# First two up-projection pairs of the feed-forward run on un-normed rows, with root and shift applied after the matmul

## The chip, the cores and the metric

The kernel runs on one core of one Trainium2 chip. The metric is the device time of one execution in microseconds (us), lower is better. Engines are named as in the profile: PE (TensorE; PEld its weight loads), DVE (VectorE), ACT (ScalarE), POOL (GpSimd), SP (SyncE, which issues the weight DMAs here).

## The reference, cut to what matters

The reference computes two transformer layers on 256 tokens of width 1024 in float32. Only the end of the second layer is touched:

```
x = x + gate_a * ((g_a * o_a + g_b * o_b) @ w_o)
h = rms_norm(x, ffn_norm) * (1.0 + scale_f) + shift_f
u = conv_width_3(h @ w_up) + b_conv          # causal, per channel, 2 * 2816 channels
val, gt = split(u, 2)
x = x + gate_f * ((silu(gt) * val) @ w_down)
```

`rms_norm` multiplies every token's row by one root, 1 / sqrt(mean of squares + eps), and every channel by a gain. The root is one number for each token, the gain times (1 + scale) and the shift one number for each channel. So `h @ w_up` equals root * ((x * gain) @ w_up) + shift @ w_up.

## The kernel before, in words

Activations lie transposed: `hT` is the residual stream as 8 tiles (KT = 8) of 128 channels x 256 tokens. Weights come as 512 KB tiles (128 x 1024) through a ring of 6 slots, `wring`, which SP fills in order; a slot is refilled once the tile six places before is done. Every float32 product is made of three faster ones. ACT rounds a weight tile into `whi` (`act_hi`, line 478, ring of 3), DVE subtracts to get the rest `wlo` (`tile_lo`, line 483, ring of 6), and PE runs upper x upper, upper x rest, rest x upper (`three`, lines 489 to 491): 24 matmuls of 256 columns for a tile. The normed activations are split likewise into `xhi`, `xlo` (both in `xboth`). POOL can run `tile_lo` too, and does so in two earlier stages.

The stage before the change is the output projection `w_o`, 8 tiles. PE makes tile t in one of 3 banks (`pe_w_o`); for each tile m DVE adds the result to `hT` (`dve_residual`, line 1662) and releases the bank (`ring_free`), ACT then rounds the weight tile three places ahead and squares `hT[m]` (`act_w_o`, lines 478 and 532), DVE makes that tile's rest (`low_ahead`), and PE sums squares over channels with a matmul against ones (`norm_sum`, line 543).

Then the norm: the last three sums; 22 matmuls on constants to keep PE busy (`pe_warm`, line 539; 44 records); ACT takes the root of the mean (`norm_act`, line 559), DVE the reciprocal (`norm_root`, 563), DVE scales 8 tiles of `hT` by it (`norm_scale`, 567), ACT applies gain and shift (571) and rounds (577), DVE makes the rests two tiles at a time (`x_rest_pair`, 597). PE starts the first up pair when the first two tiles are split (`split_pair`, called in `up_first`).

The feed-forward has FT = 22 turns. Tiles in order (F0 is the first): up pair of turn 0 (F0, F0+1), up pair of turn 1 (F0+2, F0+3), down tile of turn 0 (F0+4), up pair of turn 2 (F0+5, F0+6), down of turn 1 (F0+7), and so on. In a turn ACT copies both up results out of PSUM (`z`, 2684), DVE applies the convolution (`one`: two at 2740, four at 2748), ACT takes silu (2690), DVE multiplies value and gate into upper and rest (2758, 2759, 2761), which releases the turn's down tile on PE by the semaphore `f_w`. The engines' queues are in order, and every wait is on a semaphore written out by hand; nothing reorders work.

## Time and profile before

| | us |
|---|---|
| median of 3 runs | 1693.74 |
| range of the runs | 1693.2 to 1695.26 |
| span of the profiled execution | 1692.3 |
| median less span (what lies around it) | 1.4 |
| PE busy in the span | 1638.4 (97%) |
| DVE busy | 1244.8 (74%) |
| ACT busy | 825.3 (49%) |
| POOL busy | 157.1 (9%) |

The profile is of one execution. Times in rows count from the start of its span. In a timeline a row is: start, duration, engine, line and operation, output and inputs, shapes, count (xN: N records merged), and in brackets the idle time of that engine just before with what released it. A merged row's duration runs from the first start to the last end. Successive instructions on DVE and ACT overlap at their ends, so the step from start to start is shorter than a duration.

### The profile page before, as it was taken

To read this page: it belongs to the slowest core of one execution; us is meant where nothing else is said; L and a number is where in the kernel's file an instruction comes from. 1 tells how busy PE (TensorE), PEld (TensorE's weight loads), DVE (VectorE), ACT (ScalarE), POOL (GpSimd) and SP (SyncE) were. 2 spreads that over 40 slices of the span, in tenths; PEclk is the share of its full clock that TensorE was granted. 3 is DMA by queue.
4 is the path that set the end of the run, shared out by engine and by line. 5 is a ranking of instruction groups with operands and counts; after the bars stand their busy time and mean duration, and the time that the engine had idled before them with its cause. 6 is when DMAs were issued, how large, how long until landed. Compare 5 with 4: busy or idle time off the path is not lost.

```text
span 1692.3 us, 32795 instructions
## 1 busy us (share of the span) xinstructions
PE 1638.4 (97%) x11656; PEld 1442.0 (85%) x11656; DVE 1244.8 (74%) x2601; ACT 825.3 (49%) x1495; POOL 157.1 (9%) x131
## 2 busy tenths in 40 slices
PE   6999999999999999999999999999999988999998
PEld 4887977899988887888888888887999766899998
DVE  6885538639989888788888887887345665678887
ACT  3544011344469844555555555555444246454443
POOL 0020000007700000000000000000007203200000
PEclk9999999999999999999999999999999999999999
DMA  8742136665741388677777777776554560145553
GB/s 346 283 144 88 40 127 232 258 199 177 221 141 60 111 265 263 228 232 235 237 236 237 236 236 232 240 233 207 160 184 146 182 205 2 63 135 179 183 185 125
DMA packets 102621, 316.93 MB, mean 187 GB/s; under 512 B 11392, under 2 KB 21376, under 8 KB 102144
## 3 DMA queue, kind: packets, MB, share of 16 engines
q1 hardware_dynamic: 101664, 311.27, 56.5%
q10 hardware_dynamic: 864, 4.39, 0.7%
q8 instruction: 62, 1.02, 0.2%
q14 instruction: 31, 0.25, 0.1%
HBM read 309.71 MB, written 5.90 MB: 186 GB/s over the span
## 4 chain that ended last, share of the span: by engine, by line
PE 67%; DVE 11%; ACT 9%; issue 8%; DMA 3%; POOL 2%; DVEq 0%; SPq 0%; ACTq 0%; POOLq 0%
PE bank L489 9%; PE bank L491 9%; PE bank L490 9%; PE bank L1943 4%; PE bank L504 4%; PE bank L1945 4%; PE bank L1947 4%; PE bank L1206 3%; ACT whi L478 3%; PE bank L505 2%; ACT arena L1906 2%; PE bank L464 2%; PE bank L1492 2%; ACT arena L1897 2%; DVE xn L2065 2%
## 5 line engine op out<-in xcount | busy, mean ns | idle before, releaser
L483 DVE TENSOR_TENSOR wlo<-wring,whi 128x1024 fp32r<-128x1024 f32 x350 | 426.4, 1223 | 104.2 <-ACT whi L478 95.3
L478 ACT CAST whi<-wring 128x1024 fp32r<-128x1024 f32 x392 | 409.9, 1046 | 116.4 <-PE bank L1947 49.5
L489 PE MATMUL bank<-xboth,whi 128*128 128x256 f32 x1232 | 353.9, 287 | 7.9 <-DVE wlo L483 2.7
L490 PE MATMUL bank<-xboth,whi 128*128 128x256 f32 x1232 | 348.5, 283 | 0.0
L491 PE MATMUL bank<-xboth,wlo 128*128 128x256 f32 x1232 | 348.5, 283 | 0.0
L489 PEld LDWEIGHTS bank<-xboth,whi 128*128 128x128 f32 x1232 | 236.2, 192 | 13.1 <-issue 5.6
L490 PEld LDWEIGHTS bank<-xboth,whi 128*128 128x128 f32 x1232 | 236.3, 192 | 0.7 <-issue 0.5
L491 PEld LDWEIGHTS bank<-xboth,wlo 128*128 128x128 f32 x1232 | 236.2, 192 | 0.0
L504 PE MATMUL bank<-xboth,whi 128*128 128x512 f32 x616 | 220.8, 397 | 0.0
L483 POOL TENSOR_TENSOR wlo<-wring,whi 128x1024 fp32r<-128x1024 f32 x42 | 109.1, 2601 | 884.1 <-ACT whi L478 884.1
L505 PE MATMUL bank<-xboth,wlo 128*128 128x256 f32 x616 | 172.7, 280 | 0.0
L1943 PE MATMUL bank<-whi,Whi 128*128 128x512 f32 x512 | 159.4, 392 | 3.0 <-DVE Wlo L2048 3.0
L1945 PE MATMUL bank<-wlo,Whi 128*128 128x512 f32 x512 | 158.6, 391 | 0.0
L1947 PE MATMUL bank<-whi,Wlo 128*128 128x512 f32 x512 | 157.7, 389 | 0.0
L504 PEld LDWEIGHTS bank<-xboth,whi 128*128 128x128 f32 x616 | 115.7, 188 | 27.5
L505 PEld LDWEIGHTS bank<-xboth,wlo 128*128 128x128 f32 x616 | 116.3, 189 | 3.4
L1943 PEld LDWEIGHTS bank<-whi,Whi 128*128 128x128 f32 x512 | 95.5, 188 | 21.9 <-issue 3.9
L1945 PEld LDWEIGHTS bank<-wlo,Whi 128*128 128x128 f32 x512 | 96.1, 188 | 21.1
L1947 PEld LDWEIGHTS bank<-whi,Wlo 128*128 128x128 f32 x512 | 96.1, 188 | 21.1
L2007 ACT COPY arena<-bank 128x256 f32<-128x256 f32 x88 | 32.9, 373 | 133.6 <-PE bank L508 133.6
L2057 DVE TENSOR_TENSOR arena<-arena 128x256 f32<-128x256 f32 x88 | 56.0, 637 | 52.4 <-ACT arena L2009 52.4
L2009 ACT ACTIVATE arena<-arena 128x256 f32<-128x256 f32 x88 | 36.8, 418 | 81.7 <-DVE arena L2054 81.7
(378 smaller groups left out, 2709.0 us busy)
## 6 DMA issues: line engine op xcount, KB each, us to landing
wring<-in_w SPq DMA_DIRECT2D x463, 512.0 KB, 3.9
arena<-in_ada SPq DMA_DIRECT2D x48, 512.0 KB, 6.8
xn<-in_ada SPq DMA_DIRECT2D x96, 256.0 KB, 3.1
h_spill<-arena SPq DMA_DIRECT2D x37, 128.0 KB, 1.9
arena<-h_spill SPq DMA_DIRECT2D x37, 128.0 KB, 4.0
wring<-in_w SPq DMA_DIRECT2D x6, 384.0 KB, 4.0
wring<-in_w SPq DMA_DIRECT2D x8, 256.0 KB, 3.3
arena<-in_const ACTq DMA_DIRECT2D x1, 1215.0 KB, 5.5
```

Source lines behind the costliest of these rows:

```text
L478: act.copy(whi[:, n % HSLOTS, :], wring[:, n % SLOTS, :]).then_inc(hi_ready, 1)
L483: eng.tensor_tensor(wlo[:, n % SLOTS, :], wring[:, n % SLOTS, :], whi[:, n % HSLOTS, :].bitcast(F32), ALU.subtract).then_inc(lo_ready, 1)
L489: pe.matmul(out, h, xh, start=start, stop=False, **kw)
L490: pe.matmul(out, h, xl, start=False, stop=False, **kw)
L491: return pe.matmul(out, l, xh, start=False, stop=stop, **kw)
L504: pe.matmul(out, h, xboth[:, k, :, :], start=(k == 0), stop=False)
L505: pe.matmul(out[:, 0:S], l, xhi[:, k, :], start=False, stop=False)
L1206: mm = pe.matmul(bank[r % BANKS][:, 0:S], blocks(tile % SLOTS, k), xn[:, k, :], start=(k == 0), stop=(k == KT - 1))
L1943: pe.matmul(tok_accs[b][f][:, :], Wh, h[:, f * 512:(f + 1) * 512], start=first, stop=False)
L1945: pe.matmul(tok_accs[b][f][:, :], Wh, l[:, f * 512:(f + 1) * 512], start=False, stop=False)
L1947: mm = pe.matmul(tok_accs[b][f][:, :], Wl, h[:, f * 512:(f + 1) * 512], start=False, stop=last)
L2057: dve.tensor_tensor(ge[:, b, :], ge[:, b, :], g, ALU.mult).then_inc(w_gated, 1)
```

## The change

For turns 0 and 1 the up projection no longer waits for the norm. In the `w_o` stage ACT makes `hT[m] * gain` rounded (`raw_upper`) and DVE its rest (`raw_rest`) for each tile m, into a new buffer `raw3` with 258 columns a tile; the last two columns hold the shift, so that the matmul also gives shift @ w_up. PE runs the pairs of turn 0 (`up_first`, banks 1 and 3) and turn 1 (`up_second`, banks 0 and 2) on `raw3`; the two last `norm_sum` stand in the middle of `up_first`, and the 22 constant matmuls are gone. DVE multiplies the results by the root on the way out of PSUM (`z_scale`) and ACT adds the shift (`z_shift`). The normed rows are made after that, by one DVE instruction a tile (`norm_gain`), one on ACT (`norm_upper`) and one on DVE (`norm_rest`), between the pieces of turn 0; they are first used by turn 2. The rests of the weight tiles F0+4 and F0+5 move from DVE to POOL, and the silu table is loaded right after the root. Banks of the later turns are swapped.

```diff
@@ pe_w_o, act_w_o
-            for m in (KT - 2, KT - 1):
-                norm_sum(pe, 3, m, nsq[3])
-            pe_warm(pe, 7, 22)
         def act_w_o(act):
             for m in range(KT):
                 act.wait_ge(ring_free, RING0["w_o"] + m + 1)
+                if m == 0:
+                    raw_shift_upper(act, raw3, 9)
+                raw_upper(act, raw3, 3, m, 3 * KT)
...
+        def raw_shift_upper(act, raw, shift):
+            act.copy(raw[:, :, 0, S:RAW], wide(modc(shift, 0, KT), 2))
+        def raw_upper(act, raw, n, m, at):
+            act.activation(raw[:, m, 0, 0:S], hT[:, m, :], ACT.Identity, scale=gsc[:, n, m:m + 1]).then_inc(x_hi, 1)
+        def raw_rest(dve, raw, n, m, at):
+            dve.wait_ge(x_hi, at + m + 1)
+            dve.scalar_tensor_tensor(raw[:, m, 1, 0:S], hT[:, m, :], gsc[:, n, m:m + 1], raw[:, m, 0, 0:S].bitcast(F32),
+                                     ALU.mult, ALU.subtract).then_inc(x_lo, 1)
+        def norm_gain(dve, n, k, rt):
+            dve.scalar_tensor_tensor(xn[:, k, :], hT[:, k, :], gsc[:, n, k:k + 1], rt, ALU.mult,
+                                     ALU.mult).then_inc(x_scaled, 1)
+        def norm_upper(act, n, k, shift):
+            act.wait_ge(x_scaled, KT * n + k + 1)
+            act.activation(xhi[:, k, :], xn[:, k, :], ACT.Identity, bias=modc(shift, k)).then_inc(x_hi, 1)
+        def norm_rest(dve, k, shift, at):
+            dve.wait_ge(x_hi, at + k + 1)
+            dve.scalar_tensor_tensor(xlo[:, k, :], xn[:, k, :], modc(shift, k), xhi[:, k, :].bitcast(F32), ALU.add,
+                                     ALU.subtract).then_inc(x_lo, 1)
@@ pe_ffn
             def up_first():
                 pe.wait_ge(lo_ready, nth_split[F0 + 1])
-                split_pair(pe, (bank[0][:, 0:S], bank[0][:, S:2 * S], False), F0, 3)
+                pe.wait_ge(ring_free, RING0["w_o"] + KT - 2)
+                for k in range(KT):
+                    if k == 4:
+                        for m in (KT - 2, KT - 1):
+                            norm_sum(pe, 3, m, nsq[3])
+                    pe.wait_ge(x_lo, 12 + k + 1)
+                    for i in range(2):
+                        mm = three(pe, bank[1 + 2 * i][:, 0:RAW], F0 + i, k, raw3[:, k, 0, :], raw3[:, k, 1, :], k == 0, k == KT - 1)
...
+            def up_second():
+                pe.wait_ge(ring_free, RING0["w_o"] + KT)
+                for i in range(2):
+                    n = up_tile(1) + i
+                    pe.wait_ge(lo_ready, nth_split[n])
...
             up_first()
-            up(1, 0)
+            up_second()
             down(0, 0, first=True)
+            pe.wait_ge(x_lo, 12 + 2 * KT)
@@ act_ffn
+            def z_shift(f):
+                act.wait_ge(z_scaled, f + 2)
+                for k in range(2):
+                    ins = act.activation(zf[:, f, k, 2:258], zf[:, f, k, 2:258], ACT.Identity,
+                                         bias=z_add[:, 2 * f + k:2 * f + k + 1])
+                ins.then_inc(f_z, 1)
...
+            for k in range(4):
+                norm_upper(act, 3, k, 9)
             hi(F0 + 3, 0)
-            act.wait_ge(pad_ready, 1)
-            turn(0)
-            turn(1)
+            z_shift(0)
+            hi(F0 + 4, 0)
+            for k in range(4, KT):
+                norm_upper(act, 3, k, 9)
+            silu(0, 0)
+            hi(F0 + 5, 0)
+            z_shift(1)
+            hi(F0 + 6, 0)
+            silu(1, 0)
@@ dve_ffn
+            def z_scale(f):
+                dve.wait_ge(tile_done, up_tile(f) + 2)
+                for k in range(2):
+                    dve.tensor_tensor(zf[:, f, k, 2:258], bank[1 - f + 2 * k][:, 0:S], rtn[3], ALU.mult)
+                    ins = dve.tensor_copy(z_add[:, 2 * f + k:2 * f + k + 1], bank[1 - f + 2 * k][:, S:S + 1])
+                ins.then_inc(z_scaled, 1)
...
+                if between:
+                    between()
+                if f == 1:
+                    dve.wait_ge(lo_ready, nth_split[F0 + 5])
...
+            for k in range(4):
+                norm_gain(dve, 3, k, rtn[3])
             lo(F0 + 3, 0)
-            one(0, 0)
+            z_scale(0)
+            for k in range(4, KT):
+                norm_gain(dve, 3, k, rtn[3])
+            for k in range(4):
+                norm_rest(dve, k, 9, 4 * KT)
...
+            one(0, 0, rest)
+            z_scale(1)
             one(1, 0)
@@ scalar, vector, gpsimd programs
             act_w_o(act)
+            act_hi(act, F0 + 2, count_at(F0 + 2), None)
             norm_act(act, 3, rtn[3])
-            act_hi(act, F0 + 2, count_at(F0 + 2), None)
-            norm_shift_split(act, 3, 9)
+            act_table(act, ACT.Silu)
...
             def low_ahead(m):
                 n = FIRST["w_o"] + HSLOTS + m
...
-                if n < F0 + 1:
+                if n < F0 + 2:
                     tile_lo(dve, n, nth_split[n])
+                if m == 0:
+                    dve.wait_ge(x_hi, 3 * KT + 1)
+                    raw_shift_rest(dve, raw3, 9)
+                raw_rest(dve, raw3, 3, m, 3 * KT)
             dve_residual(dve, "w_o", 8, beside=low_ahead)
-            tile_lo(dve, F0 + 1, nth_split[F0 + 1])
+            tile_lo(dve, F0 + 2, nth_split[F0 + 2])
             norm_root(dve, v, 3, rtn[3])
-            norm_scale(dve, rtn[3])
-            for k in range(0, KT, 2):
-                x_rest_pair(dve, 3, k)
-                if k == 2:
-                    tile_lo(dve, F0 + 2, nth_split[F0 + 2])
...
+            pool.wait_ge(lo_ready, nth_split[F0 + 3])
+            for n in (F0 + 4, F0 + 5):
+                tile_lo(pool, n, nth_split[n])
```

The function called `rest` in `one(0, 0, rest)` makes `norm_rest` for the tiles 4 to 7; `one` calls it after its convolution and before the product with silu.

## Rows read from the trace of the kernel before

**Rows 1.** Windows: stretch, length, busy time of each engine (count), PEclk granted clock, DMA.

```profile
core 0: us, PE busy (x) PEld busy (x) DVE busy (x) ACT busy (x) POOL busy (x), PEclk, DMA share, GB/s
1487.30:1494.90 7.60, 6.58 (x51) 5.89 (x50) 6.83 (x12) 4.80 (x11) 0.00 (x0) 1.00 0.25 72
1526.00:1680.00 154.00, 154.00 (x1286) 154.00 (x1285) 125.42 (x216) 71.56 (x91) 0.00 (x0) 1.00 0.56 175
```

**Rows 2.** Timeline of PE from the last sums to the down tile of turn 1.

```profile
1487.25 1.03 PE L543 MATMUL bank<-arena,keep 128*128 128x256 f32 x4
...
1488.97 5.07 PE L539 MATMUL bank<-keep 128*128 128x128 f32 x44
1494.99 0.36 PE L489 MATMUL bank<-xboth,whi 128*128 128x256 f32 x1 [0.94 <-DVE xboth L597]
...
1508.77 0.39 PE L489 MATMUL bank<-Whi,whi 128*128 128x256 f32 x1 [1.66 <-DVE wlo L483]
...
1511.75 0.28 PE L489 MATMUL bank<-xboth,whi 128*128 128x256 f32 x1
...
1517.51 0.28 PE L489 MATMUL bank<-Whi,whi 128*128 128x256 f32 x1
```

**Rows 3.** Timelines of DVE and ACT, first tile of the output projection.

```profile
1465.19 0.48 DVE L1662 SCALAR_TENSOR_TENSOR hT<-bank,mod,hT 128x256 f32<-128x256 f32 x1 [0.76 <-PE bank L491]
1466.79 1.23 DVE L483 TENSOR_TENSOR wlo<-wring,whi 128x1024 fp32r<-128x1024 f32 x1 [1.11 <-ACT whi L478]
...
1465.71 1.05 ACT L478 CAST whi<-wring 128x1024 fp32r<-128x1024 f32 x1 [1.85 <-DVE hT L1662]
```

**Rows 4.** Timelines of DVE and ACT, last residual tile and norm.

```profile
1487.45 0.48 DVE L1662 SCALAR_TENSOR_TENSOR hT<-bank,mod,hT 128x256 f32<-128x256 f32 x1 [2.82 <-PE bank L491]
...
1489.68 1.75 DVE L563 RECIPROCAL arena<-arena 128x256 f32<-128x256 f32 x1 [0.48 <-ACT arena L559]
1491.47 2.77 DVE L567 TENSOR_TENSOR xn<-hT,arena 128x256 f32<-128x256 f32 x8
...
1489.17 0.47 ACT L559 ACTIVATE arena<-bank,cols 128x256 f32<-128x256 f32 x1 [0.79 <-PE bank L543]
1489.55 1.03 ACT L478 CAST whi<-wring 128x1024 fp32r<-128x1024 f32 x1
```

**Rows 5.** Timeline of DVE, turn 0 of the feed-forward.

```profile
1502.17 1.22 DVE L483 TENSOR_TENSOR wlo<-wring,whi 128x1024 fp32r<-128x1024 f32 x1 [3.02 <-ACT whi L478]
1503.31 0.73 DVE L2740 TENSOR_SCALAR arena<-arena,cols 128x256 f32<-128x256 f32 x2
1504.08 1.80 DVE L2748 SCALAR_TENSOR_TENSOR arena<-arena,cols 128x256 f32<-128x256 f32 x4
1506.36 0.43 DVE L2758 TENSOR_TENSOR Whi<-arena 128x256 fp32r<-128x256 f32 x1 [0.48 <-ACT arena L2690]
...
1507.16 0.43 DVE L2761 TENSOR_TENSOR Wlo<-arena,Whi 128x256 fp32r<-128x256 f32 x1
```

**Rows 6.** One line's instructions: durations ns min/median/max, first and last start.

```profile
L2068 DVE COPY mod<-part x96: 153/154/157, 596.1 to 1171.7; 128x1 f32 x87, 128x1 f32<-128x1 f32 x9
```

**Rows 7.** DVE line 2195, then POOL's timeline in the same stretch (1303 to 1311).

```profile
L2195 DVE SCALAR_TENSOR_TENSOR arena<-arena,cols x5: 474/1643/2628, 1303.3 to 1308.3; 128x256 f32<-128x256 f32 x5
...
1302.31 2.40 POOL L483 TENSOR_TENSOR wlo<-wring,whi 128x1024 fp32r<-128x1024 f32 x1 [3.71 <-ACT whi L478]
1305.18 2.47 POOL L483 TENSOR_TENSOR wlo<-wring,whi 128x1024 fp32r<-128x1024 f32 x1 [0.48 <-ACT whi L478]
1308.07 2.53 POOL L483 TENSOR_TENSOR wlo<-wring,whi 128x1024 fp32r<-128x1024 f32 x1 [0.42 <-ACT whi L478]
```

**Rows 8.** PE's timeline and windows (columns as in rows 1) around gaps elsewhere.

```profile
1390.83 0.90 PE L670 MATMUL bank<-keep,arena 128*128 128x128 f32 x3 [2.31 <-POOL arena L783]
1419.94 0.90 PE L670 MATMUL bank<-keep,arena 128*128 128x128 f32 x3 [1.25 <-POOL arena L783]
...
1388.00:1390.00 2.00, 0.51 (x3) 0.11 (x1) 1.89 (x12) 0.95 (x6) 0.05 (x1) 0.80 0.00 0
1394.00:1396.00 2.00, 2.00 (x11) 1.85 (x10) 0.49 (x6) 2.00 (x6) 0.57 (x2) 0.50 0.00 0
1396.00:1398.00 2.00, 2.00 (x13) 1.42 (x12) 0.91 (x7) 2.00 (x9) 0.83 (x2) 0.99 0.02 4
1422.00:1424.00 2.00, 2.00 (x13) 1.86 (x13) 0.68 (x7) 0.99 (x6) 0.33 (x1) 0.67 0.00 0
```

More of the change, by code:

```diff
@@ L166 @@
 ARENA = 41920
+RAW = S + 2
+RAW3_AT = 18736
 AFTER_WHI = S * NK + 2 * KT * S + HSLOTS * D
@@ L2634, in act_w_o, with raw_shift_rest @@
                 act_square(act, 3, m, nsq[3])
+        z_add = arena[:, RAW3_AT + 2 * KT * RAW + S:RAW3_AT + 2 * KT * RAW + S + 4]
+        def raw_shift_upper(act, raw, shift):
+            act.copy(raw[:, :, 0, S:RAW], wide(modc(shift, 0, KT), 2))
+        def raw_upper(act, raw, n, m, at):
+            act.activation(raw[:, m, 0, 0:S], hT[:, m, :], ACT.Identity, scale=gsc[:, n, m:m + 1]).then_inc(x_hi, 1)
+        def raw_shift_rest(dve, raw, shift):
+            dve.tensor_tensor(raw[:, :, 1, S:RAW], wide(modc(shift, 0, KT), 2), raw[:, :, 0, S:RAW].bitcast(F32), ALU.subtract)
+        def raw_rest(dve, raw, n, m, at):
[12 more added lines that the diff above has]
+                                     ALU.subtract).then_inc(x_lo, 1)
         f_z, f_u, f_g, f_whi, f_w = sem("f_z"), sem("f_u"), sem("f_g"), sem("f_whi"), sem("f_w")
@@ L2647, in up_first @@
                 pe.wait_ge(lo_ready, nth_split[F0 + 1])
-                split_pair(pe, (bank[0][:, 0:S], bank[0][:, S:2 * S], False), F0, 3)
+                pe.wait_ge(ring_free, RING0["w_o"] + KT - 2)
[6 more added lines that the diff above has]
+                        mm = three(pe, bank[1 + 2 * i][:, 0:RAW], F0 + i, k, raw3[:, k, 0, :], raw3[:, k, 1, :], k == 0, k == KT - 1)
+                        if k == KT - 1:
+                            mm.then_inc(tile_done, 1)
+            def up_second():
[3 more added lines that the diff above has]
+                    pe.wait_ge(lo_ready, nth_split[n])
+                    for k in range(KT):
+                        mm = three(pe, bank[2 * i][:, 0:RAW], n, k, raw3[:, k, 0, :], raw3[:, k, 1, :], k == 0, k == KT - 1)
+                    mm.then_inc(tile_done, 1)
             def up(f, i):
@@ L2724, in lo, with one @@
                     tile_lo(dve, n, 6 * i + nth_split[n])
-            def one(f, i):
+            def z_scale(f):
[4 more added lines that the diff above has]
+                ins.then_inc(z_scaled, 1)
+            def one(f, i, between=None):
                 n = turn_tile(f)
-                if f > 0:
+                if f > 1:
                     lo(n + 2, i)
@@ L2761, in one, with rest @@
                 dve.tensor_tensor(Wlo[:, b, :], Wf[:, b, :], Whi[:, b, :].bitcast(F32), ALU.subtract).then_inc(f_w, 1)
+            for k in range(4):
+                norm_gain(dve, 3, k, rtn[3])
             lo(F0 + 3, 0)
-            one(0, 0)
+            z_scale(0)
[3 more added lines that the diff above has]
+                norm_rest(dve, k, 9, 4 * KT)
+            def rest():
+                for k in range(4, KT):
+                    norm_rest(dve, k, 9, 4 * KT)
+            one(0, 0, rest)
+            z_scale(1)
             one(1, 0)
```

16 lines of the change are left out of this document (10 added, 6 removed).

## Prediction

> **What bounds the kernel now.** I read the page first: PE is busy for 97% of the span and no other engine is near that. Then the windows by stage [rows 1]. In the loop of the feed-forward PE is busy 154.0 of 154.0 us while DVE has 125.4, so a shift of PE's schedule at the entry of the loop reaches the end one for one, and nothing DVE or ACT gain inside the loop counts. The stretch at the norm is different: PE's 6.58 busy us of 7.60 are mostly filler. PE's timeline there [rows 2] shows three things. After the last `w_o` tile (its last matmul starts near 1487.1) come the sums, then 44 records on constants, and the first up matmul starts at 1494.99. Up pairs 0 and 1 run to about 1507.1. The down tile of turn 0 starts at 1508.77 after 1.66 us idle, and from then on the tiles follow without a gap: up pair 2 at 1511.75, down tile 1 at 1517.51. That last number is my meter: where down tile 1 starts is what the change moves. A tile is (1517.51 - 1511.75) / 2 = 2.88 us.
>
> So the change can win at most the 7.6 us between `w_o` and the first up tile, plus the 1.66. What it wins depends on who holds down tile 0. That is `f_w` of turn 0, which needs the root, both up results, convolution and silu. This chain lies on DVE and ACT, and the change puts more work on it.
>
> **Part 1, the raw rows in the `w_o` stage.** Before, tile m costs a loop residual, ACT rounding, DVE rest: ACT starts 0.52 us after the residual (1465.71 - 1465.19), DVE's rest starts 1.08 after ACT (1466.79 - 1465.71) [rows 3], and a following DVE instruction starts 1.14 after that (1503.31 - 1502.17) [rows 5]: 2.74 us, inside PE's 2.88 plus 0.43 for a sum. Now `raw_upper` stands between residual and rounding. An ACT instruction of this size with one per-partition operand takes a step of 0.38 (1489.55 - 1489.17) [rows 4]. `raw_rest` stands behind the weight rest. Its step is that of a convolution tap, 0.40: four take 1.80 with one dependent break [rows 5], so a pair takes about 0.88, a duration of 0.48 and a step of 0.40. The loop becomes 2.74 + 0.38 + 0.40 = 3.52 us, longer than PE's, and DVE sets the pace. With 0.25 for the shift columns in m = 0 (two instructions between a column copy's 0.15 [rows 6] and nothing), residual 6 starts at 1465.19 + 0.25 + 6 x 3.52 = 1486.6 and residual 7 at 1490.1, where before it stood at 1487.45 [rows 4]. The weight rests of the `w_o` tiles still come in time: the one for tile 7 ends near 1482.7, and PE wants it at about 1484.2. The rest of F0+1 follows residual 6: 1486.6 + 0.52 + 0.38 + 1.08 + 1.23 = 1489.8. `up_first` waits for it, so PE starts at 1489.9, 5.1 us earlier than now, after about 2.0 us of idling that used to be filled.
>
> **Part 2, the sums and the root.** Four k-steps take 2.88 us, to 1492.8; the two sums end 1.03 us later (four records, [rows 2]) at 1493.8. Square 7 is done by 1491.7 (residual 7 + 0.52 + 0.38 + some 0.7), so it isn't late. ACT's root starts at 1493.85, DVE's reciprocal 0.51 later (1489.68 - 1489.17) at 1494.35, and the first `norm_gain` 1.79 later (1491.47 - 1489.68, [rows 4]) at 1496.15. The root is thus 4.7 us later than before: it waits for the slower residual loop and for half of `up_first`. The silu table load stands beside the reciprocal and costs nothing here; it leaves a place where ACT waited anyway.
>
> **Part 3, the chain to `f_w`.** Four gains: the fourth ends at 1496.15 + 3 x 0.40 + 0.48 = 1497.85. ACT's fourth `norm_upper` starts there, rounding of F0+3 0.38 later at 1498.3 (PE has finished F0 at 1496.5), DVE's rest of F0+3 1.08 later at 1499.4, `z_scale(0)` at 1500.55. PE finishes `up_first` at 1496.5 and F0+2 at 1499.4, waits 1.2 us for that rest, and finishes F0+3 at 1503.5. `z_scale(0)` is two multiplications with a step of 0.34 (eight of line 567 take 2.77, [rows 4]) and two column copies, between 0.08 and 0.15 each [rows 6]: 0.9. Gains 4 to 7: 1.6. Rests 0 to 3: 1.6. Convolution of turn 0: 2.57 (1503.31 to 1504.08 + 1.80, [rows 5]). Rests 4 to 7: 1.6; silu is hidden beside them. Product into upper and rest: 1.23 (1506.36 to 1507.59, [rows 5]). Sum 9.5: `f_w` at 1510.1. Before it stood at 1507.6. So even with nothing in its way down tile 0 starts at 1510.2 in place of 1508.77: +1.4 us. The 96 matmuls were made early, and PE then idles from 1503.5.
>
> What is removed doesn't help: filler matmuls, 8 scalings (2.77 us), 8 ACT shifts and 4 paired rests lay ahead of PE's start, and their successors (8 gains, 8 rests of 0.40) now lie in front of `f_w`. `lo` of F0+4 leaves DVE, where it ended just before 1508.77.
>
> **Part 4, POOL's two weight rests.** POOL takes 2.40 us for what DVE does in 1.23. That alone is covered. What isn't: at 1303 DVE runs five `scalar_tensor_tensor` with two inputs in SBUF while POOL makes such rests. They take 474 ns at best, 1643 in the median, 2628 at most [rows 7]. Two pass at about 0.48, and the longest end as POOL's ends. So an instruction of this kind that meets a POOL rest is held until that is done: 2.63 - 0.48 = 2.15 us each time. The first POOL rest (F0+4) starts when ACT has rounded it: `z_shift(0)` from 1501.5, then rounding 1502.3 to 1503.4. DVE is then in the `norm_rest` row, all of that kind. F0+5 is rounded after silu(0) and starts 1.5 us after the convolution's end, just as DVE reaches the products (two SBUF inputs). Both hits lie on the chain: +4.3, so `f_w` at 1514.4 and down tile 0 at 1514.5. The bounds are 0 (DVE lies between hits) and 2 x 2.4. I take 2 x 2.15, since DVE's queue has no hole there. Later stages keep up: the rest of F0+6 is due at about 1520, PE wants it at 1520.3 or later.
>
> The Trainium skill ("GPSIMD Engine Reference", 1. Specifications) says that POOL shares its SBUF interfaces with VectorE, with contention for instructions with two SBUF inputs or in a two-port mode. By that the multiplications out of PSUM go free and the two `tensor_scalar` of a turn do not; it gives no price, and a sum by it differs only if a hit falls on those two. The skill also says ("VectorE: DVE Perf Modes", The DRAIN you can't avoid) that the next operation doesn't start until the pipe is empty, though one that isn't held starts earlier. With a full drain the 12 gains and rests behind `z_scale` would be 0.48 apart and the sum 1.0 us longer; the rows of line 567 show a step shorter than the duration, and I keep 0.40.
>
> **Part 5, the granted clock.** PE now idles 11.0 us before down tile 0 (1503.5 to 1514.5), with no filler. Elsewhere it fell to 0.50 (1.2 GHz) around gaps of 2.31 and 1.25 us with thin work before them, and came back 5.2 us after PE resumed in one case (1390.83 to about 1396) and 3.4 us in the other (1419.94 to 1423.3, from the mean of 0.67) [rows 8]. The 1.66 us gap at 1507 cost nothing. After 11 us I expect the low clock. At half speed a stretch of 3.4 to 5.2 us loses 1.7 to 2.6 us of work; I take 1.7, since the work behind this gap is dense. The bound below is 0.
>
> **Sum.** PE: 1514.5 + 3 x 2.88 + 1.7 = 1524.8 at down tile 1, against 1517.51: +7.3 us. The profiled span of 1692.3 becomes 1699.6; with the 1.44 us that the median lies above the span, 1701.1. The 258 columns in place of 256 cost 96 x 0.12 x 2/256 = 0.1 us at a place where PE waits anyway.
>
> **Rivals.**
> - *No collision with POOL.* `f_w` at 1510.1; with the clock's 1.7 it is +3.1: 1696.8 (with the clock held too, +1.4: 1695.1). For it: POOL's start depends on ACT's order within half a microsecond. Against it: DVE is without a hole from 1499.4 on. 12%. One hit alone gives 1699.
> - *The clock holds in spite of the gap*, hits as forecast: 1699.4. 10%.
> - *The clock falls at the first gap already* (1487.9 to 1489.9). `up_first` and the sums then run at half speed and the root comes about 1.5 us later: 1702.6. For it the 1.25 and 2.31 us gaps, against it the dense work ahead of this one, as at 1507. 20%.
> - *The other side: turn 0 is not what holds PE.* If the chain from the reciprocal to `f_w` were short enough to lie beside the two raw pairs, down tile 0 would follow F0+3 at 1503.5 and down tile 1 would start at 1512.1: -5.4, 1688.4. It decides from the point where `f_w` comes before 1508.7, which is 1.4 us less than my undisturbed chain and 5.7 less than the disturbed one, with the clock held. Against it stands every row of part 3. 7% for anything faster.
>
> **How the numbers follow.** The forecast case has 51%. Slower by over 0.2% (beyond 1697.1; 0.2% is about what a measurement can tell from no change) are the forecast, the second and the third rival: 0.81. Within 0.2% (1690.4 to 1697.1) the first rival: 0.12. Faster 0.07. The range leaves out the other side and most of the undisturbed clock: from 1696.0, between the variants of the first rival, to 1704.0, the forecast with the first gap's 1.5, and 1.4 for a full drain or the longer clock stretch.
>
> **What would show it.** Right: `w_o` residuals 3.5 us apart; first raw up matmul near 1490; reciprocal near 1494.4; PE idle of 10 us or more ahead of the first matmul on `Whi`; DVE instructions of `norm_rest` and of line 2758's successor with over 2 us, ending with POOL's rests; PE's clock near 0.5 behind the gap. Wrong: `Whi`'s first matmul before 1509 would break part 3; `norm_rest` all under 0.5 us would break part 4; a loop of `w_o` still at 3.3 would break part 1.

## The result, and the profile after

| | before | after |
|---|---|---|
| median, us | 1693.74 | 1700.72 (5 runs, 1698.3 to 1704.33) |
| span of the profiled execution, us | 1692.3 | 1702.5 |
| PE busy, us | 1638.4 | 1638.8 |
| DVE busy, us | 1244.8 | 1252.5 |

The ratio after to before is 1.0042, with the interval 1.0031 to 1.0053: the change makes the kernel slower, by 7.1 us (5.2 to 9.0). The forecast was 1701.1.

The profiled execution is the longest of the five, so two things have to be parted. The first residual of `w_o`, which lies ahead of nearly everything the change touches, starts at 1466.39 in it and at 1465.19 before [rows 3]: 1.2 us are from further up, where the granted clock was 0.50 from 1457.0 to 1463.8 in this execution and 1.00 in that of the kernel before. What is left is 10.2 - 1.2 = 9.0 us. From here on I count from that residual. The meter of the prediction, the start of down tile 1, stands at 1517.51 - 1465.19 = 52.3 us before [rows 2] and at 1527.69 - 1466.39 = 61.3 after. From there to the end of the span it is 174.8 us in both (1692.3 - 1517.51 and 1702.5 - 1527.69), as it is to within 0.1 us in all ten experiments below. So the loop of the feed-forward passes the shift on one for one. What scatters between executions is the part ahead: this first residual stands anywhere from 1462.15 to 1467.65 in the twelve traces, with the work ahead of it untouched. That is why medians over a few runs blur a change of 2 us which the meter shows. The meter has a limit of its own: each value is that of one execution, with the clock that this execution was granted.

The traced execution of the changed kernel isn't the typical one. Low clock shows as 0.50 in every trace here, so twice what the mean clock lacks of 1, times the span, estimates how long it was low: 34 us in the traced execution (mean clock 0.990) and 17 to 27 us in the other four (0.995 to 0.992). Which of the low stretches they lacked isn't seen, and some lie ahead of the change.

The changed loop in `w_o`, timeline of DVE in the kernel after (columns as in [rows 2]):

```profile
1466.39 0.48 DVE L1667 SCALAR_TENSOR_TENSOR hT<-bank,mod,hT 128x256 f32<-128x256 f32 x1 [0.79 <-PE bank L495]
...
1477.17 0.48 DVE L1667 SCALAR_TENSOR_TENSOR hT<-bank,mod,hT 128x256 f32<-128x256 f32 x1
1479.16 1.23 DVE L487 TENSOR_TENSOR wlo<-wring,whi 128x1024 fp32r<-128x1024 f32 x1 [1.51 <-ACT whi L482]
1480.31 0.48 DVE L2658 SCALAR_TENSOR_TENSOR raw<-hT,gsc,raw 128x256 fp32r<-128x256 f32 x1
1480.70 0.48 DVE L1667 SCALAR_TENSOR_TENSOR hT<-bank,mod,hT 128x256 f32<-128x256 f32 x1
...
1491.30 0.48 DVE L1667 SCALAR_TENSOR_TENSOR hT<-bank,mod,hT 128x256 f32<-128x256 f32 x1
```

Read the two residuals in the middle: 1480.70 - 1477.17 = 3.53 us a turn. In brackets stands why: DVE sits 1.51 us until ACT has rounded the weight tile, and ACT begins that tile only behind `raw_upper`. The loop is a circle through two engines, with each of them idle for part of it. Before, the last residual stood at 1487.45 - 1465.19 = 22.3 [rows 3, 4]; now it is at 24.9.

PE in the kernel after, the first matmul behind each gap, and the start of down tile 1 (the matmuls of a down tile read `Whi`):

```profile
1491.04 0.53 PE L493 MATMUL bank<-raw,whi 128*128 128x258 f32 x1 [2.00 <-DVE wlo L487]
...
1503.37 0.39 PE L493 MATMUL bank<-raw,whi 128*128 128x258 f32 x1 [1.03 <-DVE wlo L487]
...
1516.73 0.55 PE L493 MATMUL bank<-Whi,whi 128*128 128x256 f32 x1 [10.22 <-DVE Wlo L2846]
...
1527.69 0.28 PE L493 MATMUL bank<-Whi,whi 128*128 128x256 f32 x1
```

The three gaps of the forecast are all there, 2.0, 1.2 and 11.0 us forecast, and the last is held by the rest of the product in turn 0. The windows of the same kernel (columns as in [rows 1]) show the granted clock around them:

```profile
1490.00:1492.00 2.00, 0.96 (x4) 0.96 (x5) 1.78 (x3) 0.23 (x2) 0.00 (x0) 0.78 0.67 236
1492.00:1494.00 2.00, 2.00 (x12) 2.00 (x11) 0.82 (x2) 1.56 (x3) 0.00 (x0) 0.50 0.00 0
...
1516.73:1522.00 5.27, 5.27 (x25) 5.27 (x26) 4.22 (x12) 2.26 (x4) 0.00 (x0) 0.51 0.02 3
1522.00:1524.00 2.00, 2.00 (x19) 2.00 (x19) 1.93 (x5) 1.06 (x1) 0.00 (x0) 1.00 0.38 72
1530.00:1690.00 160.00, 160.00 (x1336) 160.00 (x1335) 131.43 (x225) 74.04 (x93) 0.00 (x0) 1.00 0.57 176
```

The eighth column is the clock. It is low (0.50, 1.2 GHz) behind the first gap as well as behind the third, which the forecast case did not have. The counts in the PE column say what that costs: 12 matmuls in 2 us against 19. The last line is the loop: PE busy for all of 160 us, as before.

DVE in the kernel after, from the reciprocal to the product, with POOL's two weight rests below:

```profile
1497.11 1.75 DVE L567 RECIPROCAL arena<-arena 128x256 f32<-128x256 f32 x1 [2.22 <-ACT arena L563]
1498.89 1.68 DVE L2663 SCALAR_TENSOR_TENSOR xn<-hT,gsc,arena 128x256 f32<-128x256 f32 x4
1502.10 1.22 DVE L487 TENSOR_TENSOR wlo<-wring,whi 128x1024 fp32r<-128x1024 f32 x1 [1.53 <-ACT whi L482]
...
1505.62 3.76 DVE L2674 SCALAR_TENSOR_TENSOR xboth<-xn,mod,xboth 128x256 fp32r<-128x256 f32 x4
...
1511.77 1.67 DVE L2674 SCALAR_TENSOR_TENSOR xboth<-xn,mod,xboth 128x256 fp32r<-128x256 f32 x4
1513.36 0.42 DVE L2843 TENSOR_TENSOR Whi<-arena 128x256 fp32r<-128x256 f32 x1
1513.69 0.42 DVE L2844 TENSOR_TENSOR arena<-arena 128x256 f32<-128x256 f32 x1
1514.14 2.44 DVE L2846 TENSOR_TENSOR Wlo<-arena,Whi 128x256 fp32r<-128x256 f32 x1
...
1506.15 2.55 POOL L487 TENSOR_TENSOR wlo<-wring,whi 128x1024 fp32r<-128x1024 f32 x1 [47.22 <-ACT whi L482]
1513.32 2.99 POOL L487 TENSOR_TENSOR wlo<-wring,whi 128x1024 fp32r<-128x1024 f32 x1 [4.62 <-ACT whi L482]
```

Line 2674 (`norm_rest`) comes twice, four instructions each: 3.76 us where the first four meet a POOL rest (1506.15 to 1508.70), 1.67 where the second four meet none. And the rest of the product (L2846) takes 2.44 us beside the second POOL rest and ends 0.27 us after it. The two instructions of the product ahead of it (L2843, L2844) also have two inputs in SBUF and start 0.04 and 0.37 us after POOL's rest, and they take their 0.42 us. So each POOL rest holds one instruction, not every one that overlaps it; among the first four of line 2674 it is one of 2.57 us.

### The profile page after: what moved, and what is told of

The parts are those of the page before. It is cut to its first block, busy times and chain, and to the rows that moved or that the text cites. A ratio compares the mean times of both kernels' runs of the same rounds, so it can differ in the third digit from the quotient of the medians.

```text
span 1702.5 us, 32727 instructions
## 1 busy us (share of the span) xinstructions
PE 1638.8 (96%) x11612; PEld 1443.0 (85%) x11612; DVE 1252.5 (74%) x2620; ACT 827.9 (49%) x1499; POOL 162.9 (10%) x133
## 4 chain that ended last, share of the span: by engine, by line
PE 70%; DVE 11%; ACT 8%; issue 6%; DMA 2%; POOL 2%; DVEq 0%; SPq 0%; ACTq 0%; POOLq 0%
PE bank L493 9%; PE bank L494 8%; PE bank L495 8%; PE bank L508 5%; PE bank L1948 5%; PE bank L1950 5%; PE bank L1952 5%; PE bank L1211 3%; PE bank L509 3%; ACT whi L482 2%; ACT arena L1911 2%; DVE wlo L487 2%; PE bank L468 2%; PE bank L1497 2%; ACT arena L1902 2%
## 5 line engine op out<-in xcount | busy, mean ns | idle before, releaser
L493 PE MATMUL bank<-xboth,whi 128*128 128x256 f32 x1200 | 344.7, 287 | 6.4 <-DVE wlo L487 2.2
L494 PE MATMUL bank<-xboth,whi 128*128 128x256 f32 x1200 | 339.6, 283 | 0.0
L495 PE MATMUL bank<-xboth,wlo 128*128 128x256 f32 x1200 | 339.6, 283 | 0.0
L493 PEld LDWEIGHTS bank<-xboth,whi 128*128 128x128 f32 x1200 | 230.4, 192 | 10.9 <-issue 4.5
L494 PEld LDWEIGHTS bank<-xboth,whi 128*128 128x128 f32 x1200 | 230.4, 192 | 0.7 <-issue 0.5
L495 PEld LDWEIGHTS bank<-xboth,wlo 128*128 128x128 f32 x1200 | 230.2, 192 | 0.0
L487 POOL TENSOR_TENSOR wlo<-wring,whi 128x1024 fp32r<-128x1024 f32 x44 | 114.7, 2610 | 935.2 <-ACT whi L482 935.2
L509 PE MATMUL bank<-xboth,wlo 128*128 128x256 f32 x616 | 172.7, 280 | 0.0
L508 PEld LDWEIGHTS bank<-xboth,whi 128*128 128x128 f32 x616 | 115.7, 188 | 27.5
L509 PEld LDWEIGHTS bank<-xboth,wlo 128*128 128x128 f32 x616 | 116.3, 189 | 3.4
L1890 PEld LDWEIGHTS bank<-arena 128*128 128x128 f32 x512 | 62.1, 191 | 14.0 <-DVE arena L1872 13.3
```

Source lines behind the costliest of these rows:

```text
L487: eng.tensor_tensor(wlo[:, n % SLOTS, :], wring[:, n % SLOTS, :], whi[:, n % HSLOTS, :].bitcast(F32), ALU.subtract).then_inc(lo_ready, 1)
L493: pe.matmul(out, h, xh, start=start, stop=False, **kw)
L494: pe.matmul(out, h, xl, start=False, stop=False, **kw)
L495: return pe.matmul(out, l, xh, start=False, stop=stop, **kw)
L508: pe.matmul(out, h, xboth[:, k, :, :], start=(k == 0), stop=False)
L509: pe.matmul(out[:, 0:S], l, xhi[:, k, :], start=False, stop=False)
```

## The experiments

All are compared on the meter: microseconds from the first residual of `w_o` to the root's reciprocal on DVE, to the first matmul of down tile 0, and to that of down tile 1. The last two columns set the timed ratio to the kernel before against what the meter says. Every meter value lies in the interval of its ratio or, for after itself, on its edge. The intervals are 3 to 6 us wide, so the meter and not the timed runs carries the sizes below.

| kernel | reciprocal | down 0 | down 1 | less before | ratio by the runs (interval), in us |
|---|---|---|---|---|---|
| before | 24.5 | 43.6 | 52.3 | | |
| after | 30.7 | 50.3 | 61.3 | +9.0 | +7.1 (5.2 to 9.0) |
| e1_dve | 30.7 | 47.3 | 58.1 | +5.8 | +6.8 (4.7 to 8.8) |
| e2_warm | 29.2 | 48.9 | 57.6 | +5.2 | +7.1 (4.2 to 10.0) |
| e3_both | 29.2 | 45.9 | 55.4 | +3.0 | +3.9 (2.2 to 5.6) |
| e4_loop | 25.8 | 45.4 | 56.1 | +3.8 | +3.7 (2.0 to 5.4) |
| e5_all | 25.8 | 42.4 | 51.9 | -0.4 | -1.2 (-2.7 to 0.3) |
| e6_order | 25.0 | 37.7 | 49.4 | -3.0 | -2.9 (-4.4 to -1.5) |
| e7_nofill | 24.5 | 44.6 | 53.3 | +1.0 | +1.2 (-0.3 to 2.9) |
| e8_v2dve | 25.0 | 38.7 | 50.3 | -2.0 | -2.9 (-4.6 to -1.4) |
| e9_order2 | 25.0 | 37.7 | 47.3 | -5.0 | -5.1 (-7.1 to -3.0) |
| e10_order3 | 25.0 | 37.8 | 47.3 | -5.0 | -3.7 (-5.4 to -2.2) |

### Do POOL's rests hold DVE? (e1_dve)

The changed kernel with the rests of F0+4 and F0+5 back on DVE:

```diff
                 for k in range(4, KT):
                     norm_rest(dve, k, 9, 4 * KT)
+                lo(F0 + 4, 0)
             one(0, 0, rest)
+            lo(F0 + 5, 0)
             z_scale(1)
...
             att_pool(pool, nsa_jobs + mla_jobs)
-            pool.wait_ge(lo_ready, nth_split[F0 + 3])
-            for n in (F0 + 4, F0 + 5):
-                tile_lo(pool, n, nth_split[n])
```

> The changed kernel, but DVE and not POOL makes the weight rests of F0+4 and F0+5 (one ahead of turn 0's product, one behind it). Measured as the distance from the first w_o residual to the start of down tile 1: 52.3 us before, 61.3 in the changed kernel's profile. If POOL's rests hold DVE (my theory, 2.0 to 2.1 us each), the norm_rest instructions are 0.48 us all of them, Wlo of turn 0 is 0.43, the chain wins 4.1 and pays 1.14 for the rest that DVE now makes: distance 58.3 with the clock falling as before, time about 3 us less. If the long instructions come from something else (DMA, ACT), they stay at over 2 us, the distance grows by 1.1 to 62.4 and the time by 1.

Down tile 1 came at 58.1. The same rows as above, DVE in e1_dve:

```profile
1506.85 1.66 DVE L2674 SCALAR_TENSOR_TENSOR xboth<-xn,mod,xboth 128x256 fp32r<-128x256 f32 x4
...
1510.91 1.67 DVE L2674 SCALAR_TENSOR_TENSOR xboth<-xn,mod,xboth 128x256 fp32r<-128x256 f32 x4
1512.49 1.22 DVE L487 TENSOR_TENSOR wlo<-wring,whi 128x1024 fp32r<-128x1024 f32 x1
...
1514.42 0.43 DVE L2846 TENSOR_TENSOR Wlo<-arena,Whi 128x256 fp32r<-128x256 f32 x1
```

The first four rests are at 1.66 and the product's at 0.43. So a POOL rest took 3.76 - 1.66 = 2.1 us and 2.44 - 0.43 = 2.0 us from DVE, where DVE gives 1.14 to make one itself. The chain from the reciprocal to down tile 0 went from 19.6 to 16.7 us, by 3.0: the two collisions' 4.1 gone, and the 1.14 of F0+4's rest, which DVE now makes at 1512.49, back in it (F0+5's comes behind the product and costs this chain nothing). Moving these rests off DVE to help DVE made its chain later. The expected 3 us in the timed runs isn't there: the ratio is 1.0040 against 1.0042, with intervals wide enough for the meter's 3.2.

What tells the held instructions from the others can be read in the kernel before, where POOL makes such rests in two earlier stages:

```profile
L2188 DVE SCALAR_TENSOR_TENSOR arena<-arena,cols,bank x6: 742/743/748, 1295.9 to 1299.2; 128x512 f32<-128x512 f32 x6
...
1296.22 2.37 POOL L483 TENSOR_TENSOR wlo<-wring,whi 128x1024 fp32r<-128x1024 f32 x1 [0.50 <-ACT whi L478]
...
L2200 DVE TENSOR_TENSOR arena<-bank,arena x7: 691/692/693, 1313.4 to 1318.4; 128x512 f32<-128x512 f32 x7
...
1313.82 2.35 POOL L483 TENSOR_TENSOR wlo<-wring,whi 128x1024 fp32r<-128x1024 f32 x1 [0.50 <-ACT whi L478]
...
L1784 DVE MATCH_REPLACE8 arena<-arena x32: 274/277/281, 382.3 to 419.4; 128x128 f32<-128x128 f32 x32
```

Lines 2188 and 2200 read one input from PSUM (`bank`) and one from SBUF; those that run wholly beside a POOL rest take as long as those that run clear of one, within 6 ns. Line 1784 reads one tensor in SBUF; 22 of its 32 run wholly beside a POOL rest, and none takes over 281 ns. The held ones, line 2195 [rows 7] and the two above, all read two tensors in SBUF.

### What do the gaps cost through the clock? (e2_warm)

The changed kernel with matmuls on constants put into two of the gaps:

```diff
+            pe_warm(pe, 7, 8)
             up_first()
             up_second()
+            pe_warm(pe, 7, 40)
             down(0, 0, first=True)
```

> The changed kernel with constant matmuls on PE in its two gaps: 8 (1.8 us) ahead of up_first, 40 (9.2 us) ahead of down tile 0. POOL's rests stay. If the fallen clock costs what the trace suggests (1.6 us at up_first, 2.5 us behind the long gap), the granted clock is 1.00 throughout the stretch, the two collisions stay, and the distance from the first w_o residual to down tile 1 is 57.2 in place of 61.3; the runs also scatter less than the changed kernel's 1698.3 to 1704.3. If the clock isn't a cost there (PE would have waited anyway), the distance stays within 1 us of 61.3.

Two windows of e2_warm, the first over the start of `up_first` and the sums, the second over down tile 0 and what follows:

```profile
1490.00:1492.00 2.00, 2.00 (x16) 1.90 (x15) 1.23 (x1) 0.47 (x2) 0.00 (x0) 1.00 0.01 4
...
1512.00:1516.00 4.00, 4.00 (x34) 4.00 (x35) 2.95 (x10) 1.84 (x3) 0.00 (x0) 1.00 0.00 0
```

The clock is full in both, and the reciprocal comes at 29.2, 1.5 us earlier than in the changed kernel's trace, though the raw rows and the weight tile come at the same time (first raw matmul 24.6 in both). From down tile 0 to down tile 1 it takes 57.6 - 48.9 = 8.7 us, as before (52.3 - 43.6), and not the 11.0 of the changed kernel. So in the profiled execution the clock cost 1.5 + 2.2 = 3.7 us. The POOL rests are still there and DVE is held as long as with the low clock (DVE in e2_warm):

```profile
1500.78 3.78 DVE L2674 SCALAR_TENSOR_TENSOR xboth<-xn,mod,xboth 128x256 fp32r<-128x256 f32 x4
...
1509.32 2.45 DVE L2848 TENSOR_TENSOR Wlo<-arena,Whi 128x256 fp32r<-128x256 f32 x1
```

The timed runs do not confirm the full 3.7: e2_warm has the ratio 1.0042 from four runs, the same as the changed kernel's, with an interval that holds its meter's 1.0031 (5.2 / 1693) too. What the runs leave open is how often an execution has the low clock behind the first gap; the five spans of the changed kernel go from 1696.5 at a mean clock of 0.995 to 1702.5 at 0.990, and only that of 1702.5 has a trace.

### Both together (e3_both)

The edits of e1_dve and e2_warm, with 26 in place of 40.

> Both edits: DVE makes the two weight rests, and constant matmuls stand in the gaps (8 and 26). Theory: the costs add, distance 61.3 - 3.0 - 4.1 = 54.2, still 1.9 more than before's 52.3, because the chain to f_w alone is 1.4 us too long and the extra rest costs 1.1: about 1695.5, ratio to before 1.001. If the two costs were the same time counted twice (the clock's loss hidden behind the collisions), the distance would be 57 or more.

Down tile 0 came at 45.9, but down tile 1 at 55.4, 1.15 us after what I expected. PE in e3_both shows a wait that was in neither of the two (below it the row of DVE that ends it):

```profile
1508.01 0.36 PE L493 MATMUL bank<-Whi,whi 128*128 128x256 f32 x1 [1.44 <-DVE Wlo L2848]
...
1514.53 0.39 PE L493 MATMUL bank<-xboth,whi 128*128 128x256 f32 x1 [0.54 <-DVE wlo L487]
...
1513.26 1.22 DVE L487 TENSOR_TENSOR wlo<-wring,whi 128x1024 fp32r<-128x1024 f32 x1
```

Now the rest of F0+6 is late: DVE makes it from 1513.26 on, behind the convolution of turn 1 and ahead of its product, and PE has been waiting since 1514.00. In e1_dve there is no such wait, with PE at the low clock behind down tile 0's start; that the low clock is what covered it is argued, not shown. The gains of the two edits add up for down tile 0 and not behind it: from down 0 to down 1 it takes 9.5 us, of which 0.54 is this wait.

### The loop of `w_o` (e4_loop)

In the changed kernel, the weight tile goes ahead of the raw rows on ACT, the raw rest of tile m-1 and not of m stands beside residual m on DVE, and the last sums stand behind the first k-step of `up_first`:

```diff
-                raw_upper(act, raw3, 3, m, 3 * KT)
                 n = FIRST["w_o"] + HSLOTS + m
                 if m < KT - 1:
                     act_hi(act, n, count_at(n), None)
...
+                if m < KT - 1:
+                    raw_upper(act, raw3, 3, m, 3 * KT)
                 act_square(act, 3, m, nsq[3])
...
-                    if k == 4:
+                    if k == 1:
                         for m in (KT - 2, KT - 1):
                             norm_sum(pe, 3, m, nsq[3])
...
+                if m > 0:
+                    raw_rest(dve, raw3, 3, m - 1, 3 * KT)
                 if n < F0 + 2:
                     tile_lo(dve, n, nth_split[n])
...
-                raw_rest(dve, raw3, 3, m, 3 * KT)
```

> The changed kernel with only the order in the w_o stage altered: ACT rounds the weight tile first and makes raw_upper after it, DVE makes raw_rest of the tile before while it waits for ACT, and the last two sums stand after the first k-step of up_first. POOL's rests and the missing filler stay. Theory: the longer residual loop (3.53 us measured) is what sets PE's start and the root: the loop falls back to PE's 3.3, up_first starts with a gap under 0.5 us, the reciprocal starts 25 to 26 us after the first residual in place of 30.7, and all of it reaches down tile 1: distance 55 to 56.5. If the root isn't what f_w waits for (but PE's tile F0+3 or its rest), the distance moves by less than 2 us.

DVE in e4_loop, residuals 6 and 7:

```profile
1483.50 0.48 DVE L1667 SCALAR_TENSOR_TENSOR hT<-bank,mod,hT 128x256 f32<-128x256 f32 x1 [0.47 <-PE bank L495]
...
1486.80 0.48 DVE L1667 SCALAR_TENSOR_TENSOR hT<-bank,mod,hT 128x256 f32<-128x256 f32 x1 [0.48 <-PE bank L495]
```

They are 3.30 us apart and released by PE's bank: PE sets the pace again, the last residual stands at 22.3 as before, and the first raw matmul at 22.3 in place of 24.6 with no gap ahead of it. The root is 4.9 us earlier than in the changed kernel's trace: 2.3 for the loop (24.65 - 22.31), 1.5 for the clock behind the first gap, and what remains, 1.1, put down to the sums further forward, which no run moved alone. The two collisions with POOL and the gap of 10.22 us ahead of down tile 0 are untouched, and the clock behind that gap is low for some 4.6 us (windows of e4_loop):

```profile
1509.93:1514.60 4.67, 4.67 (x22) 4.67 (x23) 3.62 (x11) 2.26 (x4) 0.00 (x0) 0.51 0.02 5
```

This takes 56.1 - 45.4 - 8.7 = 2.0 us.

### All three (e5_all)

The edits of e1_dve and e4_loop, and 26 matmuls on constants ahead of down tile 0 alone.

> The changed kernel with the three edits together: the w_o order of e4_loop, DVE's weight rests of e1_dve, 26 constant matmuls ahead of down tile 0. If the terms add, the reciprocal stands 25.8 us behind the first w_o residual, f_w at 45.7 - 3.4 = 42.3, down tile 0 at 42.4 and down tile 1 at 51.9 (55.35 of e3_both less 3.4): level with before (52.3). So the whole loss is in the four terms. If a further cost is hidden behind them, the distance stays over 53.5.

51.9, as expected, 0.4 us earlier than before. With the loop, the collisions and the clock taken out, the up pairs that PE makes 7.5 us earlier (first raw matmul 22.3, first up matmul before 29.8) bring 0.4 us. This is what part 3 of the prediction counted: the undisturbed `f_w` comes when it came before (42.3 and 42.4), since the gains, shifts and rests that used to lie ahead of PE's start now lie ahead of it. Down tile 0 gains 1.2 us, as it no longer waits for its weight rest behind `f_w` [rows 2], and loses most of that to the wait for F0+6 found in e3_both, here 0.53.

### Take the norm out of the chain (e6_order, e8_v2dve)

If the chain is what holds PE, the normed rows have to leave it. This is e5_all with the gains and shifts back in the old form (DVE scales two tiles at a time, ACT shifts and rounds, DVE makes rests in pairs of tiles), 4 constant matmuls ahead of down tile 0 and 6 behind it, with the rests of only four of the eight tiles between `z_scale(0)` and the product of turn 0, the others behind it; the rest of F0+2 goes to POOL, where it runs beside the reciprocal:

```diff
-            for k in range(4):
-                norm_gain(dve, 3, k, rtn[3])
-            lo(F0 + 3, 0)
+            for k in range(0, KT, 2):
+                dve.tensor_tensor(xn[:, k:k + 2, :], hT[:, k:k + 2, :], over(rtn[3], 2), ALU.mult).then_inc(x_scaled, 2)
             z_scale(0)
...
+            lo(F0 + 3, 0)
...
+            def between():
+                for k in (0, 2):
+                    x_rest_pair(dve, 4, k)
...
+            pool.wait_ge(lo_ready, nth_split[F0 + 1])
+            tile_lo(pool, F0 + 2, nth_split[F0 + 2])
```

> A rearranged version meant to beat both kernels: w_o order of e4_loop; z_scale(0) straight behind the root multiplications, which take two tiles at a time; gain and shift back on ACT; rests two tiles at a time; F0+3 rounded before the normed tiles; convolution of turn 0 ahead of all rests; POOL makes only the rest of F0+2, beside the reciprocal, which has one input. Theory (DVE's chain is what holds down tiles 0 and 1): f_w near 37.7 us behind the first residual, down tile 0 near 38, down tile 1 at 48 to 49 in place of 52.3: 4 us faster than before, ratio 0.9978. If PE or POOL set it, down tile 1 is not before 51. The reciprocal stays under 1.8 us if POOL's rest doesn't touch one-input instructions; over 3 us if it does.

Down tile 0 comes at 37.7 and down tile 1 at 49.4, 3.0 us earlier than before and 0.4 us later than the 48 to 49 expected. e8_v2dve is the same kernel with the rest of F0+2 on DVE:

> e6_order with the rest of F0+2 on DVE, behind the reciprocal, and POOL unused there. If POOL's rest beside the reciprocal is free, e6_order wins DVE 1.1 us by it, part of which DVE would have waited for F0+1 anyway: this one is 0 to 1.1 us later at down tile 1. If POOL's rest costs the reciprocal, this one is earlier.

It is 1.0 us later at down tile 0 (38.7) and at down tile 1 (50.3), so here POOL pays by the meter; the timed runs have the ratio 0.9983 for both and don't tell them apart. The rows say why this place differs from the two of the change (DVE, then POOL, in e6_order):

```profile
1487.66 1.75 DVE L567 RECIPROCAL arena<-arena 128x256 f32<-128x256 f32 x1 [0.89 <-ACT arena L563]
...
1487.34 2.41 POOL L487 TENSOR_TENSOR wlo<-wring,whi 128x1024 fp32r<-128x1024 f32 x1 [30.17 <-ACT whi L482]
```

POOL works from 1487.34 to 1489.75, over the whole of the reciprocal, and the reciprocal takes 1.75 us as it does without POOL. The reciprocal reads one tensor in SBUF, like line 1784 above.

The two traces differ in the clock as well, which fell in e8_v2dve behind the gap ahead of down tile 0 and not in e6_order behind one of 1.81 us (PE, then windows, in e8_v2dve):

```profile
1502.98 0.36 PE L493 MATMUL bank<-Whi,whi 128*128 128x256 f32 x1 [2.02 <-DVE Wlo L2859]
...
1504.00:1507.30 3.30, 3.30 (x18) 3.30 (x17) 1.53 (x3) 3.10 (x7) 0.00 (x0) 0.50 0.02 5
```

The 1.0 us stands at down tile 0 already, ahead of that stretch, and from there to down tile 1 both take 11.6 us.

### One more order (e9_order2, e10_order3)

e6_order left 0.74 us of waiting for a rest of the normed rows and 0.34 for that of F0+6, besides the 6 constant matmuls (12 records). In e9_order2 the filler behind down tile 0 is gone, ACT makes the last two normed tiles ahead of silu(1), and DVE makes the rest of F0+6 ahead of turn 1; e10_order3 also drops the 4 constant matmuls (8 records) ahead of down tile 0.

```diff
             pe.wait_ge(f_z, 1)
-            pe_warm(pe, 3, 6)
...
             shifted(4)
+            shifted(6)
             z_shift(1)
             hi(F0 + 6, 0)
-            shifted(6)
...
                 x_rest_pair(dve, 4, k)
+            lo(F0 + 6, 0)
             dve.wait_ge(x_lo, 12 + KT + 4)
             one(1, 0)
```

> e6_order with three small edits: ACT makes the last two normed tiles right behind the two before them, DVE makes the rest of F0+6 ahead of turn 1's convolution, and the six constant matmuls ahead of up pair 2 are gone. Theory (after down tile 0 DVE's order still holds PE, by 0.74 and 0.34 us in the profile, and the filler costs up to 1.4): up pair 2 follows down tile 0 without a gap, down tile 1 stands 46.9 to 47.5 us behind the first w_o residual in place of 49.4, 52.3 before; time 2 us under e6_order, ratio to before 0.997. If PE was held by something else in e6_order, it stays over 48.5.

> e9_order2 without the four constant matmuls ahead of down tile 0, so that PE idles about 1.8 us there behind dense work. If a gap of that length behind dense work leaves the granted clock at 1.00 (as the 1.66 us gap before), everything stands where it stood in e9_order2 within 0.2 us. If the clock falls, down tile 1 comes 1 to 2.6 us later.

Both put down tile 1 at 47.3. e9_order2 has a median of 1687.49 us, ratio 0.9970 (0.9958 to 0.9982); by the runs it is the best kernel of this study, ahead of both the one before and the changed one, and by the meter it is level with e10_order3. PE in e9_order2:

```profile
1500.48 0.36 PE L493 MATMUL bank<-Whi,whi 128*128 128x256 f32 x1 [1.82 <-DVE Wlo L2856]
1503.91 0.38 PE L493 MATMUL bank<-xboth,whi 128*128 128x256 f32 x1 [0.32 <-issue]
```

Down tile 0 follows 5.8 us earlier than before, counted from the first residual. The idea of the change thus pays off once the normed rows are out of turn 0's way. In e10_order3 the gap is 2.7 us without filler, not the 1.8 expected, since the removed constant matmuls had stood in it, and the clock is 1.00 in the windows around it. That is one execution: the mean clock of its ten timed runs is 0.994 to 0.996, against 0.995 to 0.998 in the six of e9_order2, so the clock may have fallen in others.

### What did the old filler buy? (e7_nofill)

The kernel before, with `pe_warm(pe, 7, 22)` taken out and nothing else.

> The kernel before without its 22 constant matmuls, nothing else. PE then idles some 6 us at the norm, behind dense work and ahead of dense work. If the fallen clock costs about what it did in the changed kernel, the granted clock is near 0.50 from inside the gap to 2 to 5 us behind its end, down tile 1 stands 1.7 to 2.6 us later, at 54.0 to 54.9, and the time is 1694.5 to 1695.5. If a gap of 6 us behind dense work doesn't bring the clock down, or DVE's chain hides the loss, the distance stays at 52.3.

I expected 54.0 to 54.9 and got 53.3. The clock did fall (PE in e7_nofill behind the gap, and the windows):

```profile
1494.28 0.55 PE L489 MATMUL bank<-xboth,whi 128*128 128x256 f32 x1 [5.85 <-DVE xboth L597]
...
1492.00:1496.00 4.00, 1.72 (x8) 1.75 (x9) 3.10 (x8) 4.00 (x11) 0.00 (x0) 0.50 0.00 0
1496.00:1498.00 2.00, 2.00 (x14) 2.00 (x14) 1.72 (x3) 1.70 (x5) 0.00 (x0) 0.66 0.00 0
```

But the low stretch behind PE's restart was short, from 1494.28 to about 1497.4 (the mean of 0.66 from 1496 to 1498), where the step from matmul to matmul goes from 0.21 back to 0.12 us: 3.1 us in place of the 3.4 to 5.2 that I had read from [rows 8]. So the 22 constant matmuls of the kernel before are worth 1.0 us by the meter, and by the runs 1.2 us with zero inside the interval.

## Why the prediction was right, step by step

The forecast set down tile 1 at 1524.8 - 1465.19 = 59.6 us from the first residual, and the trace has it at 61.3; against the median (7.1 us over before, forecast 7.3) it is closer than against the one profiled execution. So near a match is in part luck: in the trace a term of 1.5 us was missing, the chain was 0.6 us shorter than forecast and the stretch behind it 0.6 us longer, and an interval of 5.2 to 9.0 would have held a forecast of 5.5 as well as one of 8.5. What was right for its own reasons is the mechanism: a longer loop, a later root, a chain lengthened by two collisions, and a fallen clock.

- **Part 1, the loop.** 3.52 forecast, 3.53 measured; last residual 24.9 in both. The first raw matmul was forecast at 24.7 and came at 24.65, after 2.00 us idle. Right, and e4_loop shows it to be the order of the instructions on ACT and DVE, not the amount of work: with the same instructions in another order the loop costs nothing.
- **Part 2, the root.** Forecast 29.2, trace 30.7. e2_warm, where only the clock is full, gives 29.2. The sum was right for a full clock. In the profiled execution the third rival happened, the clock falling at the first gap already, and it cost the 1.5 us that the rival was given. I had 20% on it and it was there in both traces that have this gap, after and e1_dve; what the other executions did isn't seen.
- **Part 3, the chain to `f_w`.** From the reciprocal to down tile 0 the forecast had 15.8 us without collisions (1510.2 - 1494.35). The trace without its collisions has 19.6 - 2.1 - 2.0 = 15.5, and e1_dve has 16.7 with one weight rest of 1.14 in the chain, 15.5 again. With POOL the forecast was 20.2 (1514.5 - 1494.35) and the trace has 19.6. PE's wait for the rest of F0+3 was 1.03 (forecast 1.2) and the gap ahead of down tile 0 10.22 (forecast 11.0).
- **Part 4, the collisions.** 2 x 2.15 forecast, 2.1 and 2.0 measured, one on `norm_rest` and one on the product, as placed. Within the product the sign named line 2758's successor; that one (L2843) took 0.42, and the one held was the successor of line 2761 (L2846). e1_dve removes both at one stroke and shows cause and size. The row of five instructions at 1303 [rows 7] carried this well. The page of the Trainium skill named there ("GPSIMD Engine Reference", 1. Specifications) has contention for two inputs in SBUF; the traces agree for `norm_rest` and the product's rest (held), for the reciprocal (not held, e6_order) and for one input in PSUM (not held, lines 2188 and 2200). They also show two instructions with two inputs in SBUF that passed at the start of a POOL rest.
- **The drain.** The rule of the Trainium skill that I weighed ("VectorE: DVE Perf Modes", The DRAIN you can't avoid) would, taken as a full drain, have had the gains 0.48 apart, four of them 1.92 us; the same section says that a next instruction which isn't held starts earlier. They take 1.68 (line 2663), a step of 0.40, and the four rests 1.66. Keeping 0.40 was right.
- **Part 5, the clock behind the long gap.** The term of the sum that was mis-sized. I took 1.7 us from the shorter of two low stretches, 3.4 us. Here the clock was low behind the gap from 1516.73 to 1521.8, 5.1 us, and down tile 1 came 11.0 us after down tile 0 in place of 8.7: 2.2 us. In e1_dve and e4_loop it was low for 4.7 and 4.6 us and the loss 2.0. My upper bound of 2.6 held.
- **Rivals.** No collision (12%) is out by e1_dve. The clock holding (10%) is out in every trace with the 10 us gap or the 7 us gap. The other side (7%) I tied to the point where `f_w` comes before 1508.7 less 1465.19, 43.5 us: e5_all has it at 42.3 and turns to -0.4, e6_order at 37.6 and turns to -3.0. The sign fits the threshold; the size in e5_all is 0.8 short of the 1.2 that it would give, and the wait for F0+6 took most of that. The price given for it, -5.4, took the chain as short enough to lie beside both raw pairs. No run tests it: e9_order2 comes to -5.0 with the chain still 1.8 us late, but PE starts 2.4 us earlier there (22.3 in place of 24.7).
- **One step that wasn't tested by the change:** "later stages keep up". In the changed kernel no such wait is seen. In e3_both, with down tile 0 4.5 us earlier, the rest of F0+6 made PE wait.

## What to carry to other kernels

Work that is taken off the front of an engine that waits must not be put behind it, in the chain that ends the next wait; ask where every postponed instruction goes, and sum the chain to the next release before counting what starts earlier. Count moved work by what it meets at its new place: a weight rest put on POOL cost DVE nothing beside instructions with at most one tensor in SBUF, and two microseconds where it held one with two, which is more than DVE would have taken to make it. Where the change sits in a small part of a long kernel, find a meter inside the trace (here from the last untouched instruction to the first one of the steady loop), because the scatter of whole runs is larger than the effect.
